# Folding seven feature tiles into one column before the ones-products of three norms

## What is computed

```
def layer_norm(x, g, b):
    mu = jnp.mean(xf, -1, keepdims=True)
    xc = xf - mu
    var = jnp.mean(xc * xc, -1, keepdims=True)
    return xc * lax.rsqrt(var + LN_EPS) * g + b
...
x = layer_norm(DEEPNORM_ALPHA * x + (1 + g1) * mixer(u), ...)
...
x = layer_norm(DEEPNORM_ALPHA * x + (1 + g2) * ffn(u), ...)
```

## Time and profile before

| | us |
|---|---|
| runs (three) | 1143.23, 1139.75, 1141.96 |
| median | 1141.96 |
| the profiled execution, its own time | 1143.53 |
| its span in the trace | 1141.8 |
| mean granted TensorE clock | 0.988 |
| TensorE busy in the span | 1086.2 |
| VectorE busy | 742.5 |
| ScalarE busy | 556.8 |

### The profile page before, as it was taken

The page is one execution under the profiler, slowest core; times in us unless marked ns, Lnnn a source line. Parts: engine busy times, 40 slices in busy tenths (PEclk is TensorE's granted clock), DMA queues, the critical chain, the costliest instruction groups (busy, mean ns, idle before and its releaser), DMA issues. The chain is left out here.

```text
span 1141.8 us, 31042 instructions
## 1 busy us (share of the span) xinstructions
PE 1086.2 (95%) x12796; PEld 817.9 (72%) x12796; DVE 742.5 (65%) x1612; ACT 556.8 (49%) x1014; POOL 179.4 (16%) x277
## 2 busy tenths in 40 slices
PE   6999899899999999999999999999999999989996
PEld 3566789878999999766769878866666777533433
DVE  1575855876444444577774777765786786687657
ACT  2252333436343433246324333568778677567553
POOL 8000004000000000000002200122322222554220
PEclk9998999999999999999999999999999999999998
DMA  9846693587554454635377347299999999999871
GB/s 307 302 138 243 215 296 118 218 292 233 159 174 156 158 162 157 222 112 180 117 225 227 112 152 265 94 379 381 381 387 386 354 346 362 376 335 359 299 270 43
DMA packets 172931, 276.72 MB, mean 242 GB/s; under 512 B 7893, under 2 KB 105199, under 8 KB 167672
## 3 DMA queue, kind: packets, MB, share of 16 engines
q1 hardware_dynamic: 160768, 264.01, 66.5%
q10 hardware_dynamic: 12024, 10.73, 3.2%
HBM read 268.42 MB, written 6.30 MB: 241 GB/s over the span
## 5 line engine op out<-in xcount | busy, mean ns | idle before, releaser
L2142 ACT COPY CP<-XW 128x512 f32 (+1 forms) x487 | 252.1, 593 | 117.0 <-PE bank L1727 50.6
L2932 DVE COPY CP<-XW 128x512 f32 (+1 forms) x470 | 196.9, 463 | 91.5 <-PE bank L1727 37.8
L1082 POOL COPY CP<-XW 128x512 f32 (+1 forms) x163 | 119.0, 741 | 352.3 <-PE bank L1727 182.1
L1727 PE MATMUL bank<-CP,UG 128*32 128x256 f32 (+2 forms) x2816 | 168.5, 380 | 3.7 <-issue 3.5
L2301 DVE TENSOR_TENSOR lo<-raw,hi 128x2048 fp32r<-128x2048 f32 (+1 forms) x42 | 95.8, 2281 | 85.9 <-ACT hi L2088 48.7
L1727 PEld LDWEIGHTS bank<-CP,UG 128*32 128x32 f32 x2816 | 99.4, 110 | 54.5 <-issue 7.8
L1067 POOL TENSOR_TENSOR SD<-SD,EG 128x512 f32<-128x512 f32 x16 | 24.2, 1548 | 567.9 <-PE bank L1448 567.9
L1269 PE MATMUL bank<-UM,raw 128*128 128x288 f32 x416 | 108.2, 416 | 0.0
L1094 PE MATMUL bank<-UH,hi 128*128 128x288 f32 x352 | 104.6, 297 | 2.3 <-DVE UL L2289 2.0
L1095 PE MATMUL bank<-UH,lo 128*128 128x288 f32 x352 | 103.8, 295 | 0.0
L1096 PE MATMUL bank<-UL,hi 128*128 128x288 f32 x352 | 103.5, 294 | 0.0
(11 more groups left out here) (494 smaller groups left out, 2071.6 us busy)
## 6 DMA issues: line engine op xcount, KB each, us to landing
raw<-in_w_ada_dram SPq DMA_DIRECT2D x48, 1024.0 KB, 7.0
XW<-in_w_exp_down_dram SPq DMA_DIRECT2D x44, 1024.0 KB, 8.7
XW<-in_w_exp_gate_dram SPq DMA_DIRECT2D x32, 1024.0 KB, 9.6
XW<-in_w_exp_up_dram SPq DMA_DIRECT2D x32, 1024.0 KB, 9.1
raw<-in_w_in_dram SPq DMA_DIRECT2D x28, 1024.0 KB, 8.9
XW<-in_w_exp_gate_dram SPq DMA_DIRECT2D x16, 768.0 KB, 7.3
XW<-in_w_exp_up_dram SPq DMA_DIRECT2D x16, 768.0 KB, 8.4
raw<-in_w_ff_gate_dram SPq DMA_DIRECT2D x11, 1024.0 KB, 5.4
```

The lines of the kernel that those rows point to most:

```text
L1082: pool.tensor_copy(weights(s_, NE + j).unsqueeze(1), XW[:, s_ % RING, bass.ds(unit[j], 1), 0:width(s_)]).then_inc(S("pool_copied"), 1)
L1727: mm = pe.matmul(bank[t][UNIT * g_:UNIT * g_ + UNIT, at_:at_ + n_], UG[:, k_, UNIT * u:UNIT * u + UNIT], w_[:, q, :, :], start=(k_ == 0 an ...
L2142: act.copy(weights(s_, NE + j).unsqueeze(1), XW[:, s_ % RING, bass.ds(unit[j], 1), 0:width(s_)]).then_inc(S("act_copied"), 1)
L2932: dve.tensor_copy(weights(s_, NE + j).unsqueeze(1), XW[:, s_ % RING, bass.ds(unit[j], 1), 0:width(s_)]).then_inc(S("dve_copied"), 1)
```

## The change

The four products of each sum become two. `XSUM[0]` and `XSQ[0]` take in everything up to tile 6: after the second pair `add_up` folds the two columns into one, and a new function `add_seventh` adds tile 6 and its square. TensorE multiplies `XSUM[0]`, `XSQ[0]`, `xT[7]` and `XSQ[7]` in this order. `add_up` for tiles 4 and 5 moves ahead of tile 6's addition in norms 0 and 2 (from (3, 1) to (3, 0)), in norm 0 also ahead of `low`. On ScalarE the squares of tiles 4 and 5 move ahead of `hi_part` in norm 0, and in norm 1 the square of tile 6 moves from `lnm` to the end of the FFN's step, which is ahead of the copy of `adas` (L1864).

```
# TensorE, lnm
                     fill(base, 7)
-                    if s[2] == 1:
-                        pe.wait_ge(S("x_added"), 2)
                     pe.wait_ge(S("norm_dve"), norm_count(NORM_DVE, which, "sum"))
                     sum_part(0, XSUM[:, 0, :], first=True)
-                    sum_part(0, XSUM[:, 1, :])
-                    if s[2] == 0:
-                        pe.wait_ge(read[0], base[0])
-                    sum_part(0, xT[:, 6, :])
+                    pe.wait_ge(S("norm_dve"), norm_count(NORM_DVE, which, "sum_squares"))
+                    sum_part(1, XSQ[:, 0, :], first=True)
                     pe.wait_ge(S("x_added"), (1, 3, 4)[which])
                     sum_part(0, xT[:, 7, :], last=True).then_inc(full[6], 1)
-                    pe.wait_ge(S("norm_dve"), norm_count(NORM_DVE, which, "sum_squares"))
-                    sum_part(1, XSQ[:, 0, :], first=True)
-                    sum_part(1, XSQ[:, 1, :])
-                    pe.wait_ge(S("x_squared"), 5 * which + 4)
-                    sum_part(1, XSQ[:, 6, :])
                     pe.wait_ge(S("x_squared"), 5 * which + 5)
                     sum_part(1, XSQ[:, 7, :], last=True).then_inc(full[7], 1)
# ScalarE, wo
                     if s[2] > 0 and s[3] == 0:
+                        for b in (0, 1):
+                            act.wait_ge(read[b], base[b])
+                        squares(2 * s[2] - 2, 2)
                         if s == ('wo', 0, 3, 0):
...
                             hi_part(m + 1)
-                        for b in (0, 1):
-                            act.wait_ge(read[b], base[b])
-                        squares(2 * s[2] - 2, 2)
# ScalarE, lnm
                     if s[2] == 0:
                         act.wait_ge(read[0], base[0])
-                    else:
-                        act.wait_ge(S("x_added"), 2)
-                    squares(6, 1)
+                        squares(6, 1)
# ScalarE, end of ffn
+                    act.wait_ge(S("x_added"), 2)
+                    squares(6, 1)
# VectorE, add_up
-                op = dve.tensor_tensor(XSUM[:, :, :], ..., xT[:, v, :], ALU.add)
+                then(dve.tensor_tensor(XSUM[:, :, :], ..., xT[:, v, :], ALU.add))
                 if q == 2:
-                    op.then_inc(S("norm_dve"), 1)
+                    then(dve.tensor_tensor(XSUM[:, 0, :], XSUM[:, 0, :], XSUM[:, 1, :], ALU.add))
                 dve.wait_ge(S("x_squared"), 5 * which + q + 1)
-                op = dve.tensor_tensor(XSQ[:, 0:2, :], XSQ[:, 0:2, :], XSQ[:, v, :], ALU.add)
+                then(dve.tensor_tensor(XSQ[:, 0:2, :], XSQ[:, 0:2, :], XSQ[:, v, :], ALU.add))
                 if q == 2:
-                    op.then_inc(S("norm_dve"), 1)
-                else:
-                    then(op)
+                    then(dve.tensor_tensor(XSQ[:, 0, :], XSQ[:, 0, :], XSQ[:, 1, :], ALU.add))
+
+            def add_seventh(which):
+                dve.tensor_tensor(XSUM[:, 0, :], XSUM[:, 0, :], xT[:, 6, :], ALU.add).then_inc(S("norm_dve"), 1)
+                dve.wait_ge(S("x_squared"), 5 * which + 4)
+                dve.tensor_tensor(XSQ[:, 0, :], XSQ[:, 0, :], XSQ[:, 6, :], ALU.add).then_inc(S("norm_dve"), 1)
# VectorE, wo
-                        if s == ('wo', 0, 3, 0):
-                            low(SPLITS[m + 1][0], m + 1, 0, 0)
-                        if s[2] > 1 and t == 1:
+                        if s[2:] in ((2, 1), (3, 0)):
                             dve.wait_ge(read[0], base[0])
                             dve.wait_ge(read[1], base[1])
                             add_up(2 * l, s[2] - 1)
+                        if s == ('wo', 0, 3, 0):
+                            low(SPLITS[m + 1][0], m + 1, 0, 0)
+                        if s[2:] == (3, 1):
+                            dve.wait_ge(read[0], base[0])
+                            add_seventh(2 * l)
                         got(base, b)
# VectorE, ffn, down projection
                             if (cb, t) == (3, 1):
+                                dve.wait_ge(S("x_added"), 2)
+                                add_seventh(1)
                                 dve.wait_ge(S("ffn_mm"), 2 * UP_CB + 3 * cb + 3)
```

More of the change, by code:

```diff
@@ L2274, in add_up @@
                 v = slice(2 * q, 2 * q + 2)
-                op = dve.tensor_tensor(XSUM[:, :, :], xT[:, 0:2, :] if q == 1 else XSUM[:, :, :], xT[:, v, :], ALU.add)
+                then(dve.tensor_tensor(XSUM[:, :, :], xT[:, 0:2, :] if q == 1 else XSUM[:, :, :], xT[:, v, :], ALU.add))
                 if q == 2:
-                    op.then_inc(S("norm_dve"), 1)
+                    then(dve.tensor_tensor(XSUM[:, 0, :], XSUM[:, 0, :], XSUM[:, 1, :], ALU.add))
                 dve.wait_ge(S("x_squared"), 5 * which + q + 1)
-                op = dve.tensor_tensor(XSQ[:, 0:2, :], XSQ[:, 0:2, :], XSQ[:, v, :], ALU.add)
+                then(dve.tensor_tensor(XSQ[:, 0:2, :], XSQ[:, 0:2, :], XSQ[:, v, :], ALU.add))
                 if q == 2:
-                    op.then_inc(S("norm_dve"), 1)
-                else:
-                    then(op)
+                    then(dve.tensor_tensor(XSQ[:, 0, :], XSQ[:, 0, :], XSQ[:, 1, :], ALU.add))
[3 more added lines that the diff above has]
+                dve.tensor_tensor(XSQ[:, 0, :], XSQ[:, 0, :], XSQ[:, 6, :], ALU.add).then_inc(S("norm_dve"), 1)
             def u_low(l, q):
```

## The result

The changed kernel is slower, by about half a per cent. Its median over 20 runs is 1143.48 us (1139.83 to 1151.86); the kernel before, now also over 20 runs, has 1137.62 us (1134.23 to 1143.23). The ratio is 1.0046, 95% interval 1.003 to 1.0062, so +5.2 us against a forecast of -0.35 and "no change". The absolute time lies inside the stated range, 1139.0 to 1144.0, by luck: the three runs shown of the kernel before (median 1141.96) happened to be slow ones of it. As a change, the forecast was wrong. The profiled execution took 1143.34 us, its span 1141.6. Of the 30 runs of the kernel before that stand beside the second group of experiments, one took 2775.86 us and is left out of the ratios.

What follows compares the result with a forecast made beforehand. The prediction took a DMA and rounding to bound norm 0, VectorE's own work to limit norm 1, and products to matter in norm 2. 0.0 - 0.1 - 0.25 = -0.35 us gave 1141.6 us, range 1139.0 to 1144.0.

Steps and rivals of the forecast that it cites:

- Rival B: TensorE's clock falls behind longer pauses in the norms; up to 1.7 us a fall, three give 1146.7 us; chance 0.25.
- The three terms of the sum: Changes forecast for the norms: 0.0 us in norm 0, -0.1 in norm 1, -0.25 in norm 2.
- The products and what they are worth: Twelve of 24 leave TensorE, 5.8 us of its time; the mean comes 0.1 us earlier in norm 1, 0.25 in norm 2.
- The new additions: Four VectorE additions of 128x288 in each norm, taken as 0.46 us each, bounds 0.19 and 0.72.
- Norm 0: A DMA and a ScalarE rounding set it; the later mean is hidden: 0.0 us, bounds 0 and +0.4.
- Norm 1's moved square: Tile 6's square waits for the last FFN block, tile 7 comes 0.9 us late; mean still -0.1 us, bounds -0.6 and +0.5.
- The price: One clock fall costs up to 1.7 us, from 24 products in the experts' stage taking 4.48 us where 2.79 had done.
- The lower bound of -1.3 us: Lower end of the whole forecast change with the terms' bounds; the upper end was +1.0 us.

Runs made afterwards that it cites:

- the second group of experiments: Four kernels on another chip, against the kernel before: changed kernel alone, with four-product fills, with eight and an earlier square, kernel before with two-product fills; 1.0069, 1.0049, 1.0002, 1.0021.
- fill_early: Changed kernel with eight unread products in both pauses and norm 1's tile 6 square ahead of ScalarE's last FFN wait: 1137.07 us, ratio 1.0002 to the kernel before.
- norm 1 alone: Kernel before with the four products left out on TensorE in norm 1 only: 1144.72 us, ratio 1.0036.
- the second chip: The changed kernel run unchanged on another chip, against the kernel before there: 1144.31 us against 1138.03 us, ratio 1.0069.
- norm 0 alone: Kernel before with the four products left out on TensorE in norm 0 only: 1142.44 us against 1139.90 us, ratio 1.0018.
- norm 2 alone: Kernel before with the four products left out on TensorE in norm 2 only: 1138.05 us, ratio 0.9981.
- all three at once: Kernel before with the four products left out on TensorE in all three norms, VectorE and ScalarE untouched: 1143.31 us, ratio 1.005.
- fill_norm2: Changed kernel with eight unread products in norm 2's pause only, against the kernel before: 1147.31 us (6 runs), ratio 1.0075.
- fill_half: Changed kernel with four unread products in each pause of norms 1 and 2, against the kernel before: 1143.09 us, ratio 1.0049.

## Why the prediction was wrong, and where it was right

*The step that failed.* The sum of the forecast, 0.0 - 0.1 - 0.25 = -0.35 us, has no term for TensorE's clock. Rival B held that term and got 0.25 in all. The three terms of the sum came out as forecast; the missing one is what was measured. Its account stands below, under rival B.

*The products and what they are worth.* Right. Twelve are gone; the mean in norms 1 and 2 starts 0.16 and 0.24 us earlier (forecast 0.1 and 0.25), and VectorE still needs 1.95 us from mean to variance (475.81 to 477.76).

*The new additions.* Right: 0.46 us each for 288 columns, the middle value. The prediction had it from LNM, which reads a PSUM bank and is not such an addition; no row gave it that the two would be alike. By the rule of the Trainium skill ("VectorE: DVE Perf Modes", TRN2 errata) the estimate is 0.457 us, and the trace agrees with its 0.46.

*Norm 0.* Right, 0.00 us. The mean is later by 0.32 us (249.51 + 2.34, the shift between the two executions, is 251.85 against 251.53), the rounding waits for its DMA, and the variance and the first FFN product come when they came before.

```profile
249.44 1.91 ACT L1808 ACTIVATE hi<-raw 128x2048 fp32r<-128x2048 f32 x1 [0.29 <-DMA raw<-in_w_ff_up_dram]
251.25 0.43 ACT L2066 ACTIVATE MSQ<-LNM 128x288 f32<-128x288 f32 x1
```

*Norm 1's moved square.* Right: VectorE stood 1.53 us ahead of the seventh addition, and the copy of `adas` came late; against the kernel before the mean was still 0.16 us earlier. The late square did cost something: in fill_early, which has it ahead of the wait, the mean comes 0.33 us earlier still.

```profile
473.17 0.46 DVE L2278 TENSOR_TENSOR XSQ<-XSQ 128x288 f32<-128x288 f32 x1 [1.53 <-ACT XSQ L1822]
```

*Rival B, the clock.* The mechanism was named, with its places and pauses (forecast 2.2 and 2.2 us, measured 2.10 and 2.06; in norm 0 forecast 2.4, measured two pauses of 0.93 and 1.15, since the spin products there wait for the variance, which I had overlooked). What failed above all is its chance. I gave one or two falls 0.20 and let them come in some executions only; the runs show a fall in norm 1 in five of five traces with that pause and in norm 2 in three of three. Even so the range went only to 1144.0, while two falls by my own price give 1145.0. I took the pause alone as the measure, between 1 us (harmless) and 3 us (a fall), and did not count what TensorE does around it, nor look for the falls that the trace of before already had. Two of them come behind pauses of 1.06 us; the first of these is

```profile
94.31 1.79 PE L1380 MATMUL bank<-Tboth,MT 32*32 32x32 f32 x64 [1.06 <-DVE QKV L2470]
```

with this granted clock behind it:

```profile
95.00:98.00 3.00, 3.00 (x45) 1.86 (x46) 2.47 (x7) 0.00 (x0) 0.00 (x0) 0.50 0.85 289
```

In norm 1 the pause follows 1.2 us of transposes of 24 and 16 rows. Whether these transposes are what makes norm 1 fall at 1.88 us, while norm 2 with dense products ahead did not at 1.58, was not tried.

The price, 1.7 us each from one row of the experts' stage, was about right for norm 2 (1.5 to 1.6) and for norm 1 in three traces (1.5), and too low for norm 1 in the other two (2.6 to 2.7), where half clock lasted through the second group of projections. With two falls in every execution it gives 3.4 - 0.35 = 3.05 us, so with a right chance the forecast would have been +3, not -0.35. Leaving the products out in norm 1 alone costs 0.36% (0.10 to 0.62).

The rule of the Trainium skill cited there ("TensorE: Matmul & The Clock Gate", Part 1) says that the clock drops to half after an idle stretch. The traces agree on the drop to half. That falls would come in some executions only is not what the section says of such a pause; it was my own conclusion, and for the unfilled pauses of 1.88 us and more in norm 1 no trace shows it.

*The base and the bounds.* The three runs shown had a median 4.3 us above the 20-run median, and the profiled execution had falls of its own in the solves and the experts' stage. I took the drift as 3.5 us and should have asked what goes with it: in the runs of before, time and mean granted clock are correlated at 0.78 to 0.87. The lower bound of -1.3 us is also wrong as a sum: the bounds of the three terms add up to -0.9 (0, -0.6 and -0.3).

**What stays open.** The two norms of the changed kernel's trace cost 2.48 + 1.39 = 3.9 us; the ratio says 5.2 (3.4 to 7.1), on the second chip 7.9 (5.1 to 10.6). For the first chip that may be all, for the second the rest is not located. The parts are too uncertain to say more: norm 1 alone 0.36%, norm 0 alone 0.18% (unclear), norm 2 alone -0.19% (unclear), together 0.35%, all three at once 0.50%, each to about 0.25 either way. Why fill_norm2 is the slowest of all (0.75%) is not explained. fill_half costs 0.49% with pauses of 1.01 and 1.17 us and no fall in its trace; its slower executions were not profiled.

## What to carry to other kernels

Removing work from TensorE where another engine's chain sets the end saves little; it lengthens a pause, and TensorE's clock can fall in or behind the pause, onto work that is on the path. Before such a change, list for each place the pause that it leaves, what stands ahead of it and whether the work behind it is hidden; where it isn't, keep the engine busy with unread products up to the wait (here eight of 128x128, about 2 us, in both places: with them +0.02% against before, without them +0.69%, on one chip). Take a base time and its clock from many runs, not three.

## What the hardware showed that I had not expected

A pause of 1.88 to 2.10 us behind small transposes came with half clock in norm 1 in all five traces that have one; the shortest pause with a fall behind it that I had used was 2.98 us, though the same trace has falls behind 1.06 us. Whether the fall begins inside the pause or behind it changes its cost from 2.6 or 2.7 to 1.5 us. Products placed to hold the clock up do not do so if they stand behind the pause: in norm 2 they ran mostly at 1.2 GHz themselves, 4.32 us in place of 2.69, and the first router product waited for them.
